# Attention of a hybrid decoder step: slot probabilities are turned and copied behind the prompt's logits and exponentials of their sub-step

## Reference, cut to what matters

```python
logits = jnp.einsum('bthd,btkhd->bhtk', q, k_sel) * ATTN_SCALE + bias
p = jax.nn.softmax(jnp.where(dist >= 0, logits, -1e30), axis=-1)
out = jnp.einsum('bhtk,btkhd->bthd', p, v_sel)      # prompt and samples alike
x = x + concat([a, b]) @ w_out                       # then the MLP
```

## Time and profile before

| | |
|---|---|
| median of 3 runs | 1740.41 us (1740.24 to 1743.44) |
| the profiled execution's own time | 1743.57 us |
| its span, first to last instruction | 1741.8 us |
| PE busy | 1670.2 us, 96% of the span |
| DVE, ACT, POOL busy | 856.2, 658.3, 584.0 us |
| mean granted TensorE clock | 0.989 of full speed |

### The profile page before, as it was taken

The page is one execution under the profiler, slowest core; times in us unless marked ns, Lnnn a source line. Parts: engine busy times, 40 slices in busy tenths (PEclk is TensorE's granted clock), DMA queues, the critical chain, the costliest instruction groups (busy, mean ns, idle before and its releaser), DMA issues.

```text
span 1741.8 us, 29296 instructions
## 1 busy us (share of the span) xinstructions
PE 1670.2 (96%) x11176; PEld 1382.7 (79%) x11176; DVE 856.2 (49%) x2081; ACT 658.3 (38%) x1382; POOL 584.0 (34%) x715
## 2 busy tenths in 40 slices
PE   6899999999979999998999999999999999999997
PEld 5653464599956666665556999999999999999997
DVE  4482889987746667775214523232232323232424
ACT  4575887588225444444211221122121222222123
POOL 1100333457643777765211304040222222130500
PEclk9999999999989999999999999999999999999999
DMA  8210302225797777767600011110201011111102
GB/s 252 60 49 27 125 32 77 58 86 172 219 325 232 220 211 211 210 187 238 228 0 0 1 49 49 41 57 0 96 0 65 31 48 48 48 48 48 61 1 103
DMA packets 78184, 174.84 MB, mean 100 GB/s; under 512 B 10426, under 2 KB 26542, under 8 KB 77824
## 3 DMA queue, kind: packets, MB, share of 16 engines
q1 hardware_dynamic: 56704, 101.69, 17.2%
q0 software_dynamic: 21376, 71.75, 13.7%
HBM read 152.53 MB, written 20.88 MB: 100 GB/s over the span
## 4 chain that ended last, share of the span: by engine, by line
PE 83%; DVE 7%; issue 5%; DMA 3%; ACT 1%; DVEq 0%; SPq 0%; POOL 0%
PE psum L1897 7%; PE psum L1910 7%; PE psum L1898 7%; PE psum L1896 7%; PE psum L1908 7%; PE psum L1909 7%; PE psum L1837 7%; PE psum L1615 3%; PE psum L1463 3%; PE psum L1464 3%; PE psum L1465 3%; PE psum L1732 2%; PE psum L1420 2%; PE psum L1770 2%; PE psum L1640 2%
## 5 line engine op out<-in xcount | busy, mean ns | idle before, releaser
L1896 PE MATMUL psum<-n_hi,wup_hi 128*128 128x384 f32 (+1 forms) x768 | 251.4, 327 | 0.0
L1897 PE MATMUL psum<-n_lo,wup_hi 128*128 128x384 f32 (+1 forms) x768 | 250.9, 327 | 0.0
L1898 PE MATMUL psum<-n_hi,wup_lo 128*128 128x384 f32 (+1 forms) x768 | 250.9, 327 | 0.0
L1908 PE MATMUL psum<-h_hi,wdn_hi 128*128 128x384 f32 (+1 forms) x768 | 250.9, 327 | 0.0
L1910 PE MATMUL psum<-h_hi,wdn_lo 128*128 128x384 f32 (+1 forms) x768 | 250.2, 326 | 0.0
L1909 PE MATMUL psum<-h_lo,wdn_hi 128*128 128x384 f32 (+1 forms) x768 | 250.1, 326 | 0.0
L2543 DVE TENSOR_TENSOR h_lo<-h_full,h_hi 128x384 fp32r<-128x384 f32 (+1 forms) x96 | 112.3, 1182 | 261.7 <-ACT h_hi L1299 253.0
L1291 ACT ACTIVATE hrelu<-psum 128x384 f32<-128x384 f32 (+1 forms) x96 | 45.5, 474 | 501.6 <-PE psum L1898 501.6
L2548 DVE TENSOR_TENSOR x_region<-psum,x_region 128x384 f32<-128x384 f32 (+1 forms) x192 | 102.8, 535 | 252.9 <-PE psum L1910 251.8
L981 POOL TENSOR_TENSOR wup_lo<-wup_full,wup_hi 128x4096 fp32r<-128x4096 f32 x8 | 72.3, 9039 | 423.0 <-ACT wup_hi L1275 423.0
L1151 ACT ACTIVATE arena<-x_region,arena 128x384 bf16<-128x384 f32 (+2 forms) x192 | 166.5, 872 | 6.1 <-POOL arena L908 6.1
(11 more groups left out here) (330 smaller groups left out, 3017.8 us busy)
## 6 DMA issues: line engine op xcount, KB each, us to landing
wup_full<-in_w_up SPq DMA_DIRECT2D x8, 2048.0 KB, 8.1
wdn_full<-in_w_down SPq DMA_DIRECT2D x8, 2048.0 KB, 7.7
arena<-in_x_prompt SPq DMA_DIRECT2D x16, 512.0 KB, 10.5
arena<-k_scratch SPq DMA_DIRECT2D x32, 256.0 KB, 4.1
arena<-in_w_in SPq DMA_DIRECT2D x3, 2048.0 KB, 8.1
arena<-in_w_in SPq DMA_DIRECT2D x12, 512.0 KB, 5.8
k_scratch<-arena SPq DMA_DIRECT2D x24, 256.0 KB, 2.9
out<-arena SPq DMA_DIRECT2D x17, 256.0 KB, 3.4
```

Source lines behind the costliest of these rows:

```text
L1896: pe.matmul(b, wu_hi[:, k, col], n_hi[:, k, o:o + w], start=(k == 0), stop=False)
L1897: pe.matmul(b, wu_hi[:, k, col], n_lo[:, k, o:o + w], start=False, stop=False)
L1898: i = pe.matmul(b, wu_lo[:, k, col], n_hi[:, k, o:o + w], start=False, stop=(k == KT - 1))
L1908: pe.matmul(b, wd_hi[:, f, col], h_hi[:, hf, 0:w], start=(f == 0), stop=False)
```

## The change

In both engines' lists the two calls for the samples' probabilities move towards the end of the sub-step: on ACT behind `even_turn` and `exp`, on PE behind `values`, `turn`, `fold`, `near_logits`, `k_logits` and `logits`, and still ahead of `near_vals` and `vals`. No instruction is added, removed or resized, and the sub-step of each stays what it was. DVE's, POOL's and SP's lists are untouched.

```diff
@@ ACT, the loop over u @@
                 if b < DB and x == 1:
                     near_evac(b)
-                if u in NEAR_AT:
-                    near_p(NEAR_AT[u])
-                if u in TURN_AT:
-                    slot_p(*TURN_AT[u])
                 p, t = divmod(u - PLAG, 4)
...
                 if t == 3 and 0 <= p < NPR:
                     exp(p, 1)
+                if u in NEAR_AT:
+                    near_p(NEAR_AT[u])
+                if u in TURN_AT:
+                    slot_p(*TURN_AT[u])
                 if u - 1 in LAST_LOGIT:
@@ PE, the loop over u @@
                 if b < DB and x == 1:
                     near_turn(b)
-                if u in NEAR_AT:
-                    near_p_turn(u, NEAR_AT[u])
-                if u in TURN_AT:
-                    p_turn(u, *TURN_AT[u])
                 p, t = divmod(u - PLAG, 4)
                 if t == 0 and 2 <= p < NPR + 2:
                     values(p - 2)
...
                 if 0 <= p < NPR and t in (0, 2) and t // 2 < NCHUNK[p]:
                     logits(p, t // 2)
+                if u in NEAR_AT:
+                    near_p_turn(u, NEAR_AT[u])
+                if u in TURN_AT:
+                    p_turn(u, *TURN_AT[u])
                 if u in NEARV_AT:
```

## The result

The changed kernel takes 1748.14 us (median of 6 runs, 1745.15 to 1748.58) beside 1740.88 us for the kernel before (6 runs, 1739.38 to 1743.44): ratio 1.0041, 95% interval 1.003 to 1.0052, so +7.3 us, with 5.2 to 9.1 us from the interval. The forecast was +9.9 us and 1750.3 us, range 1745.4 to 1757.4. The profiled execution took 1748.16 us, its span is 1746.2 us.

A forecast was written before the change was run, and what follows sets the result against it. PE's own order was taken to bound the attention loop, with some 23 us of holes left. Terms 14.25 - 4.93 - 0.24 + 0.8 = +9.9 us on 1740.4 gave 1750.3 us, range 1745.4 to 1757.4.

The forecast's parts named there:

- PE, slot turns: Moving `p_turn` behind `turn` and `logits` on PE gains nothing alone; the exponential comes 0.22 us sooner.
- ACT, slot copies: `slot_p` behind `exp(p, 0)` comes late, so `vals` on PE waits: 14.25 us of new idle time.
- the 18 slots: Of 32 slot turns, those left without enough cover, where `vals` would wait for the copy; 14.25 us together.
- The formula: Wait per slot: exponential's start - 0.22 + its duration + 0.38 (copy) + 0.05 (hand-over) - start of `vals` now.
- The term that was off is the start of `vals` now: When `vals` starts on PE in the trace before the change, subtracted in each slot's wait; 742.64 us in one example.
- No refund: DVE's lateness moves along with PE, so none of the 14.25 us of stalls is given back.
- `near_p_turn`: -4.93 us: At x = 5, `turn` and `k_logits` run in PE's wait for DVE's `take_values`, saving 4.93 us.
- Clock: +0.8 us: New PE stalls may lower the granted clock; half a fall of 1.7 us counted, between none and three.
- The last sub-steps: -0.24 us, and 0 behind 814 us: Sub-step 129's slot turn waits less, 0.24 us; behind 814 us the output weights' transfer decides, so 0.
- The weight loads: `vals`' load starts after the copy; were it pulled ahead during the stall, the sum would lose 2 us.
- Faster: Rival: the exponential comes forward enough that `slot_p` ends before `vals`; 1735.2 us, chance 0.04.
- refund: Rival: DVE catches up during the stalls and its waits shrink, taking back about 9 us; 1741.3 us, chance 0.05.

The follow-up runs named there:

- even_act: Against the kernel before, only ACT's 27 slot copies at t = 2 move behind the exponential, PE keeps its order; 1758.41 us, ratio 1.0093.
- even_only: Against the kernel before, only the 27 slot turns and copies at t = 2 move, on PE and ACT; 1753.0 us, ratio 1.0062.
- odd_only: Against the kernel before, only turns and copies at sub-steps with u % 4 other than 2 move to the end; 1735.66 us, ratio 0.9966.
- vals_later: The changed kernel with `vals` of even tiles one sub-step later, behind the next `k_turn`; 1738.27 us, ratio 0.9984 to the kernel before.
- copy_mid_2: On chip 14, odd_only with t = 2 slot turns behind `turn`, copies between `even_turn` and `exp`; ratio 0.998 to the kernel before.
- odd_vals_later: odd_only with `vals` of even tiles one sub-step later; ratios to the kernel before 1.0187 on chip 5 and 1.0224 on chip 14.

## Why the prediction was right

The time came out +7.3 us where +9.9 was forecast. Both mechanisms, the copy that comes too late and the hole that is filled, are the ones forecast. The terms one by one:

**PE, slot turns: nothing by themselves.** Right for PE. Their other use, the lead of 0.22 us that they give the exponential, is seen in even_act, which is without it: 13 leads of 0.22 would be 2.9 us, and twelve slots there cost 2.8 us more than in even_only.

**ACT, slot copies: 14.25 us.** Right in mechanism: the 18 slots cost 14.0 us (the 14.1 in the expectation of even_only reads the last slot at its weight load). The formula met every one of the two-chunk j = 1 and 2 slots within 0.03 us. Two groups were off in opposite ways, so that the sum fits better than its parts is luck. The first two one-chunk slots cost 0.44 instead of 0.23 and 0.24 each: the exponential there started 0.18 and 0.52 us after ACT was free, waiting for DVE's maximum, so it had no lead. The four two-chunk j = 0 slots, with `near_vals` ahead of `vals`, cost 0.00, 0.05, 0.28 and 0.40 us, each some 0.15 less than worked out. The term that was off is the start of `vals` now. In the trace of before its first pieces run among the last of `near_vals` (L1697), as at x = 6 of tile 6:

```profile
731.72 0.39 PE L1697 MATMUL psum<-arena 128*32 128x256 f32 x2
731.75 0.79 PE L1713 MATMUL psum<-arena 128*32 128x256 f32 x6
...
732.47 1.09 PE L1615 MATMUL psum<-arena 128*128 128x128 f32 x8
```

The next `k_turn` follows 0.72 us after 731.75, and so in all four of these slots, where it follows the start of `vals` by 0.55 to 0.57 us in the others. So 0.15 us of what looked like `vals` was `near_vals`.

**No refund.** Right to 0.7 us of 14.0, which came back further on.

**`near_p_turn`: -4.93 us.** Right in mechanism, 12% too large: -4.35 us. Each but the first gave 0.11 to 0.13 us less than the work that fits the hole. Most of that is at the seam: what stands behind L1673 starts 0.34 us after it now (728.48 against 728.14), where `turn` or `k_logits` started 0.24 to 0.25 us after it before (725.84 against 725.60).

**Clock: +0.8 us.** Wrong. Up to 829 us the stage has the same single fall of the granted clock as before, behind the same wait of 1.99 us, and none behind the new stalls, where the matmuls stand up to 1.4 us; the window's mean is 0.99 in both. The step that failed is the price put on half a further fall. Further falls do occur in even_act, but as even_only shows, stalls of that length don't always bring them. Where the clock did differ is behind the stage, and the prediction has no term for it: see the next point.

**The last sub-steps: -0.24 us, and 0 behind 814 us.** Somewhat too small. The first matmul of the output projection comes 6.21 us later than in the earlier trace rows, which is 8.03 us against the loop's start, so 0.9 us of the +8.95 was regained by then:

```profile
852.50 1.88 PE L1837 MATMUL psum<-arena 128*128 128x384 f32 x5 [1.63 <-DMA arena<-in_w_out]
```

From that matmul to the end the changed kernel's execution takes 893.7 us, that of before 895.5. Most of the 1.8 us lies in these matmuls of L1837 (118.1 instead of 119.6 us from first to last), and there it is the clock: the kernel before has waited 2.26 us for the output weights and then runs at the lower level, the changed kernel has waited 1.63 us and does not (windows, before and then after):

```profile
846.00:848.00 2.00, 1.71 (x3) 1.11 (x4) 0.00 (x0) 0.00 (x0) 0.00 (x0) 0.50 0.98 347
848.00:850.00 2.00, 2.00 (x5) 1.12 (x5) 0.00 (x0) 0.00 (x0) 0.00 (x0) 0.68 1.07 402
```

```profile
852.00:854.00 2.00, 1.50 (x5) 0.97 (x6) 0.00 (x0) 0.00 (x0) 0.00 (x0) 1.00 0.94 247
```

odd_only, which waits 3.40 us there, has the low clock too, vals_later with 1.47 us has not. Forecast to result: 9.9, less 0.8 for the clock in the stage, less some 0.4 in the loop, less 0.7 in the last sub-steps, is 8.0 at the output projection, and 6.2 at the end of these two executions. The medians say 7.3, and the interval of 5.2 to 9.1 holds both. How often the clock falls there in executions that were not traced is not known.

**The weight loads.** The rule of the Trainium skill that the prediction names ("TensorE: Matmul & The Clock Gate", section "Architectural detail: the array is 16× 32×32, not 1× 128×128"), that weight loads can be pulled ahead of matmuls in flight, would have made it 2 us less. The load of `vals` starts 0.06 us after the copy's end (746.01 against 745.95) and is not drawn ahead of the wait, so the row's reading stands.

**Rivals.** Faster and refund needed the copy to be in time or DVE to catch up; 20 waits, and 9.5 us at L1640 where 10.0 stood, rule both out.

## What to carry to other kernels

Before an instruction is moved in an engine's list, compare two times of the same trace for each place: when what it is moved behind ends, and when its user starts. A short copy whose user is near must not stand behind a long operation that itself waits for a third engine; moving work into a hole where its engine is already waiting is the same edit and pays. One change can hold both, and then the split by place, not by engine, finds the good half.

## What the runs showed of the hardware

The difference between chips was not expected: the kernel before took 1817 us on chip 5 and 1805 us on chip 14 instead of 1741 us, and one of its 23 executions on chip 5 took 2068.79 us. The loss is in the attention stage, where the gathers run. From the first `k_turn` to the output projection copy_mid_2 on chip 14 takes 427 us and odd_only on chip 9 takes 356; the rest of the two differs by 4 us, the other way. A stretch of odd_only on chip 9, then of copy_mid_2 on chip 14, and of odd_vals_later, which its edit slows as well, on chip 5:

```profile
560.00:780.00 220.00, 209.77 (x2440) 141.14 (x2439) 156.77 (x554) 104.50 (x224) 164.74 (x165) 0.99 0.71 211
```

```profile
560.00:800.00 240.00, 203.94 (x2136) 132.34 (x2128) 133.69 (x483) 87.70 (x196) 144.43 (x144) 0.93 0.60 175
```

```profile
560.00:800.00 240.00, 191.10 (x1939) 121.42 (x1938) 119.38 (x439) 82.44 (x187) 127.45 (x128) 0.89 0.54 159
```

In copy_mid_2 DMA moves 175 instead of 211 GB/s with its engines less busy (0.60 against 0.71), PE is busy 85% instead of 95%, and the granted clock is 0.93 instead of 0.99. Engines that are less busy and yet late speak of a longer way for each gather and not of a full one, with four ring places to cover it. The median of a gather of keys from issue to landing fits that, 4.4 us in copy_mid_2 and 4.2 in odd_vals_later, 3.8 to 4.0 us in the traces of chip 9, but they don't say why it is longer, and whether the chip or something else at that time made it so was not tested. What is shown is that moving `vals` one sub-step back was nearly free on one chip (in vals_later) and stands 2% above the kernel before on two others (in odd_vals_later), so an order that frees ring places early is worth keeping even where it measures nothing.
